# Late cells of a Winograd feed-forward: two tile pairs finished elsewhere, and the last result added on the chip

## The reference

```
def causal_dwconv(x, past, w, b):
    ...
    for k in range(width):
        y = y + w[k] * xp[:, k:k + t]
    return y, xp[:, -(width - 1):]
...
    x = x + jnp.concatenate([o_a, o_m, o_b], axis=-1) @ w_out
    up = rmsnorm(x, g_ffn) @ w_up
    up, f_conv_new = causal_dwconv(up, f_conv_past, conv_f_w, conv_f_b)
    val, gt = jnp.split(up, 2, axis=-1)
    x = x + (jax.nn.gelu(gt) * val) @ w_down
```

## Time and profile before

| what | us |
|---|---|
| median of 3 runs | 2377.11 (2375.92 to 2377.87) |
| the profiled execution, device time | 2379.29 |
| its span, first to last instruction | 2377.5 |
| PE busy | 2320.7 (98%) |
| DVE busy | 1780.0 (75%) |
| ACT busy | 1130.8 (48%) |
| POOL busy | 399.9 (17%) |

### The profile page before, as it was taken

How to read it: one execution, slowest core, us unless ns; L and a number is a source line. 1 busy time by engine, 2 the same in 40 slices (tenths; PEclk the granted TensorE clock), 3 DMA queues, 4 the chain that set the end, 5 groups by cost and what they waited for, 6 DMA issues and landing times.

```text
span 2377.5 us, 45151 instructions
## 1 busy us (share of the span) xinstructions
PE 2320.7 (98%) x18194; PEld 2294.1 (96%) x18194; DVE 1780.0 (75%) x2284; ACT 1130.8 (48%) x1776; POOL 399.9 (17%) x313
## 2 busy tenths in 40 slices
PE   6799999999999999999999999999999899999998
PEld 6799999999999999999999999999999899999998
DVE  7877655655423698888888888888888878787875
ACT  4465433433422355555455555555555545454543
POOL 6500000000022201211112111121211221112121
PEclk9899999999999999999999999999999999999999
DMA  7523333333343343443434434344445568676854
GB/s 231 161 81 83 87 93 99 87 91 92 119 145 110 98 118 115 140 121 109 139 115 131 124 116 130 119 129 121 130 121 156 152 175 209 158 203 169 206 134 89
DMA packets 481733, 309.33 MB, mean 130 GB/s; under 512 B 10744, under 2 KB 459896, under 8 KB 481544
## 3 DMA queue, kind: packets, MB, share of 16 engines
q1 hardware_dynamic: 472824, 288.86, 41.3%
q0 software_dynamic: 8720, 17.83, 4.6%
HBM read 255.23 MB, written 53.51 MB: 130 GB/s over the span
## 4 chain that ended last, share of the span: by engine, by line
PE 91%; DVE 6%; issue 1%; ACT 1%; DMA 1%; POOLq 0%; SPq 0%; DVEq 0%; ACTq 0%
PE out L2358 20%; PE out L2360 20%; PE out L2359 20%; PE out L2064 9%; PE out L2065 9%; PE out L2067 9%; DVE xl L1459 1%; PE out L2200 1%; PE out L2143 1%; DVE ring_l L1793 1%; PE out L2158 1%; DVE wl L1449 1%; DMA raw<-in_w_mem_kv 1%; DVE t L1786 0%; DVE fl L2006 0%
## 5 line engine op out<-in xcount | busy, mean ns | idle before, releaser
L1793 DVE TENSOR_TENSOR ring_l<-pair,ring_h 128x1024 fp32r<-128x1024 f32 (+1 forms) x384 | 453.6, 1182 | 177.1 <-ACT ring_h L1273 177.1
L1273 ACT CAST ring_h<-pair 128x1024 fp32r<-128x1024 f32 (+1 forms) x384 | 383.3, 998 | 325.3 <-DVE pair L1811 240.1
L2064 PE MATMUL out<-xh,wh 128*128 128x272 f32 (+1 forms) x1792 | 504.2, 298 | 29.4 <-DVE xl L1459 25.2
L2065 PE MATMUL out<-xl,wh 128*128 128x272 f32 (+1 forms) x1792 | 488.8, 290 | 0.0
L2358 PE MATMUL out<-t,ring_h 128*128 128x272 f32 x1536 | 445.0, 290 | 6.8 <-DVE ring_l L1793 3.4
L2360 PE MATMUL out<-t,ring_l 128*128 128x272 f32 x1536 | 444.7, 290 | 0.0
L2359 PE MATMUL out<-t,ring_h 128*128 128x272 f32 x1536 | 442.6, 288 | 0.0
L2358 PE MATMUL out<-fh,ring_h 128*128 128x272 f32 x1344 | 390.2, 290 | 7.5 <-DVE fl L2006 3.2
L2360 PE MATMUL out<-fh,ring_l 128*128 128x272 f32 x1344 | 388.7, 289 | 0.0
L2359 PE MATMUL out<-fl,ring_h 128*128 128x272 f32 x1344 | 387.6, 288 | 0.0
L2067 PE MATMUL out<-xh,wl 128*128 128x272 f32 (+1 forms) x1792 | 384.2, 290 | 0.0
(11 more groups left out here) (242 smaller groups left out, 3927.6 us busy)
## 6 DMA issues: line engine op xcount, KB each, us to landing
pair<-in_w_up SPq DMA_DIRECT2D x192, 512.0 KB, 3.9
raw<-in_w_in SPq DMA_DIRECT2D x36, 1024.0 KB, 5.5
pair<-in_w_down SPq DMA_DIRECT2D x64, 384.0 KB, 4.5
pair_d<-in_w_down SPq DMA_DIRECT2D x64, 384.0 KB, 4.7
h_forms<-fb SPq DMA_DIRECT2D x24, 816.0 KB, 6.0
fr<-h_forms SPq DMA_DIRECT2D x24, 816.0 KB, 6.3
out_yT<-stage POOLq DMA_DIRECT2D x31, 544.0 KB, 8.5
raw<-in_w_out SPq DMA_DIRECT2D x16, 1024.0 KB, 5.8
```

The costliest lines, as they stand in the source:

```text
L1273: nc.scalar.copy(ring_h[:, n % 3, 0:width(i)], weight_of(p, i)).then_inc(op_hi, 1)
L1793: v.tensor_tensor(ring_l[:, n % 3, 0:w], weight_of(p, i), ring_h[:, n % 3, 0:w].bitcast(F32), ALU.subtract).then_inc(op_lo, 1)
L2064: mm(dst, w_high, hs, start=first, stop=False)
L2065: mm(dst, w_high, ls, start=False, stop=False)
```

## The change

It has four parts.

1. The value half of pair 46 (`scale_val`, `tap_f(.., 0)`, `conv_f(.., 0)`, `make_h`) leaves cell 47 and goes to cells FT + 1 and FT + 2, with `make_t` for it on POOL in cell FT + 2. In cell 47, form 1 is now split at step 2 instead of step 1.
2. The chain of pair 47 goes one cell later and its end to the end of a cell: `scale_gate`, `scale_val` and the gate's `tap_f` in FT + 3, gate convolution and gelu in FT + 4, value convolution and `make_h` at the end of FT + 5, `make_t` on POOL in FT + 5 behind `make_s3`.
3. Forms 8 and 9 are split in cells FT + 6 (step 0) and FT + 7 (step 0) instead of FT + 5 and FT + 6 (step 5), and form 10 at step 1 instead of step 0 of FT + 7. SP stores `fb` at the end of its cell FT + 6 and loads form 9 right behind it, where before it stored in FT + 5 and loaded at the head of FT + 6.
4. The last cell's output is added in SBUF: SP reads that part of y back (`y_rest`) in cell 74, DVE adds it while it copies PSUM (`kept_with_y`, four operations that take the place of ACT's `keep_a`, `keep_b`, `keep_c`, `read_c21`), and SP stores the sums with three plain transfers in place of POOL's two accumulating ones.

```
-            steps = [(e - 1, 6), (e, 1), (e, 3), (e, 6), (e + 1, 0), (e + 1, 2), (e + 1, 3)]
+            steps = [(e - 1, 6), (e, 2), (e, 3), (e, 6), (e + 1, 0), (e + 1, 2), (e + 1, 3)]
+        if c == 1:
+            steps[1:4] = [(e - 1, 0), (e, 0), (e, 1)]
...
-                if nears == 1:
+                if nears == 1 and g > FT + PAIRS_D:
                     load_form(first + 2)
...
-                if g == FT + 5:
+                if g == FT + 3:
+                    store_b11(FT - 2)
+                if g == FT + 6:
                     store_forms(FT - 1)
+                    load_form(first + 2)
+                if g == FT + PAIRS_D:
                     sp.wait_ge(f_kept, 2 * FT)
...
+                if g == CELLS - 6:
+                    d = CELLS - FT - 1 - PAIRS_D
+                    sp.wait_ge(y_out[1], 16 * (d // 2 + 1))
+                    sp.dma_start(y_rest[:], two_tiles(d)).then_inc(y_back, 16)
+            i = CELLS - 1
+            dst, src = two_tiles(i - FT), stage[(i - FT) % 2]
+            sp.wait_ge(c11_read, i + 1)
+            sp.dma_start(dst[:, 0, 0:HALF], src[:, 0, 0:HALF]).then_inc(last_out, 16)
...
+            sp.wait_ge(c12_read, i + 1)
+            sp.dma_start(dst[:, 0, HALF:ROWS], src[:, 0, HALF:ROWS]).then_inc(last_out, 16)
...
             for g in range(CELLS - 1):
-                if 2 <= g < FT + 1:
+                if 2 <= g < FT:
                     make_t(g - 2)
-                if g == FT + 5:
-                    make_t(FT - 1)
                 if g > FT:
                     add_to_y(g - 1)
                 make_s3(g + 1)
+                if g == FT + 2:
+                    make_t(FT - 2)
+                if g == FT + 5:
+                    make_t(FT - 1)
...
+            def kept_with_y(p, kept, tile, half, ready):
+                i = CELLS - 1
+                dve.wait_ge(product, at(p, i) + 1)
...
+                v.tensor_tensor(kept, x_bank(i), y_rest[:, tile, half * HALF:(half + 1) * HALF], ALU.add
+                                ).then_inc(ready, 1)
...
-                elif g == FT + 4:
-                    conv_f(FT - 1, 0)
-                    make_h(FT - 1)
...
                 make_s4(g + 1)
+                if g == FT + 2:
+                    conv_f(FT - 2, 0)
+                    make_h(FT - 2)
+                if g == FT + 5:
+                    conv_f(FT - 1, 0)
+                    make_h(FT - 1)
                 lo_form(g, 6)
```

More of the change, by code:

```diff
@@ L248, in encoder @@
                  over("stage1", [P, 2, ROWS], x_at + 5 * slot_size)]
-        assert u_at + slot_size <= rows_at + KT * ROWS * 4 and 5 * slot_size + 8 * ROWS <= 8 * form
+        y_rest = over("y_rest", [P, 2, ROWS], u_at + slot_size)
+        assert u_at + slot_size + 8 * ROWS <= rows_at + KT * ROWS * 4 and 5 * slot_size + 8 * ROWS <= 8 * form
         xc, ga, gi, dec, tan = (rows[:, n, :] for n in range(5))
@@ L375, in encoder @@
         y_out = [sem("y_out0"), sem("y_out1")]
+        y_back = sem("y_back")
+        last_out = sem("last_out")
         small_out = sem("small_out")
@@ L446, in tiles_of, with two_tiles @@
             return first, first + 4
+        def two_tiles(d):
+            first, second = tiles_of(d)
+            return yT.rearrange("(k p) n -> p k n", p=P)[:, first:second + 1:second - first, :]
         def x_bank(i):
@@ L775, in _ @@
                     refill(g, 1)
-                if g % 2 and g < FT:
-                    if g == FT - 1:
-                        store_forms(g - 2)
+                if g == FT - 1:
+                    store_forms(g - 2)
+                elif g % 2 and g < FT:
                     store_b11(g - 1)
@@ L925, in add_to_y @@
                     pool.wait_ge(y_out[d % 2], 16 * (d // 2))
[L926 to L934, removed]
+                pool.wait_ge(c11_read, i + 1)
+                pool.wait_ge(c12_read, i + 1)
+                pool.wait_ge(c21_read, i + 1)
+                pool.wait_ge(c22_read, i + 1)
+                nc.gpsimd.dma_start(two_tiles(d), stage[d % 2][:], accum_op=ALU.add).then_inc(y_out[d % 2], 16)
             for g in range(CELLS - 1):
-                if 2 <= g < FT + 1:
+                if 2 <= g < FT:
                     make_t(g - 2)
-                if g == FT + 5:
-                    make_t(FT - 1)
                 if g > FT:
@@ L1275, in keep_a @@
             def keep_a(i):
+                if i == CELLS - 1:
+                    return
                 act.wait_ge(product, at(1, i) + 1)
@@ L1412, in _ @@
                     gelu_f(g - 1)
+                if g < FT - 1:
                     tap_f(g - 1, 0)
-                elif g == FT + 2:
+                elif g == FT + 1:
+                    tap_f(FT - 2, 0)
+                elif g == FT + 3:
                     tap_f(FT - 1, 1)
-                elif g == FT + 3:
+                elif g == FT + 4:
                     gelu_f(FT - 1)
@@ L1429, in _ @@
             g = CELLS - 1
-            hi_op(7, g)
-            keep_b(g)
-            hi_op(4, g)
-            keep_c(g)
-            hi_op(3, g)
-            read_c21(g)
+            for p in (7, 4, 3):
+                hi_op(p, g)
         @block.vector
@@ L2007, in lo_form @@
                                 ).then_inc(form_lo, 1)
+            def kept_with_y(p, kept, tile, half, ready):
+                i = CELLS - 1
+                dve.wait_ge(product, at(p, i) + 1)
+                if p != 4:
+                    dve.wait_ge({1: c11_read, 6: c12_read, 7: c22_read}[p], i)
+                dve.wait_ge(y_back, 16)
+                if p == 4:
+                    dve.wait_ge(y_out[(i - FT) % 2], 16 * ((i - FT) // 2))
+                v.tensor_tensor(kept, x_bank(i), y_rest[:, tile, half * HALF:(half + 1) * HALF], ALU.add
+                                ).then_inc(ready, 1)
             for g in range(1, CELLS - 1):
@@ L2017, in _ @@
                 lo_op(7, g)
-                if g < FT:
+                if g < FT - 1:
                     scale_val(g - 1)
-                elif g == FT + 2:
+                elif g == FT + 1:
+                    scale_val(FT - 2)
+                elif g == FT + 3:
                     scale_val(FT - 1)
@@ L2050, in _ @@
             lo_op(4, g)
+            kept_with_y(6, kept_b[:], 0, 1, b_kept)
             lo_op(3, g)
+            kept_with_y(7, kept_c[:], 1, 1, c_kept)
             read_c22(g)
+            kept_with_y(4, stage[(g - FT) % 2][:, 1, 0:HALF], 1, 0, c21_read)
             read_c12(g)
```

18 lines of the change are left out of this document (11 added, 7 removed).

## The result

The changed kernel takes 2387.43 us, median of 6 runs (2386.21 to 2388.97), against 2377.56 for the kernel before (6 runs). The ratio is 1.0043, 95% interval [1.0030, 1.0056]: 9.9 us slower. The forecast was 2378.8 with a range to 2384, so it was wrong, and on the side of its second rival. The profiled execution took 2388.21 us with a span of 2386.4.

The account below looks back on a forecast made before the run. PE's matmuls are 91% of the chain, so only PE's waits could change. Gains of 11.5 us against costs of 13.2 made it 1.7 longer, 2378.8 us predicted from the 2377.11 median, range 2372 to 2384.

Parts of the forecast that it names:

- second rival: ACT's cast of form 9 in FT + 7: slower store and load, wait 12.2 us, total 2382.7; chance 0.23.
- Part D: Form 9 loaded behind the store: PE waits 8.3 us at product 7 of FT + 7, clock 1.4; cost 9.7.
- part A: Seam at cell 47: DVE bounds it, form 3 starts 3.1 us sooner; gain 4.2, bounds 2.5 and 5.5.
- B: Cell FT + 4: the 2.09 us wait and its clock loss go, product 6 waits 0.7; gain 3.0.
- C: Moved work's new places, ends of FT + 2 and FT + 5: new PE waits; cost 3.5, bounds 2 and 5.
- part E: The end: plain stores from SP, POOL's drain already over; gain 4.1 us, bounds 2.8 and 4.6.
- third rival: The seam yields little: DVE filled by forms 3 to 6 and POOL's s3, gain 2.5, total 2380.5; chance 0.10.
- The 0.2 for forms 8 and 9: Cells after FT + 4: forms 8 and 9 no longer at step 5 of the next two cells; gain 0.2 us.
- Mostly hidden: Rival on the wait for form 9: 3 us or less remains, clock unhurt, total 2371.6; chance 0.22.

Follow-up runs that it names:

- e5: Changed kernel with SP's cell FT + 6 transfers in the order ACT needs: store of fb, form 9, form 10, form 11; 2381.98 us.
- e4: Kernel before with only the change's last part: last cell's additions in SBUF and plain stores; 2373.55 us.
- e1: Kernel before with only SP's store of fb moved to the end of FT + 6 and form 9's load behind it; 2390.14 us.
- e7: Changed kernel with pair 47's second convolution, make_h and make_t one cell earlier, SP's former order, and form 1 at step 1 of cell 47; 2374.15 us.
- e9: Changed kernel with store and form 9's load ahead of forms 10 and 11, and POOL's y additions of FT + 5 and FT + 6 cut to two columns; 2378.38 us.
- e8: Changed kernel with POOL's y additions of cells FT + 5 and FT + 6 cut to two columns; 2383.65 us.

## Why the prediction was wrong

**Part D was mis-sized, not misplaced.** The forecast named the store, the load, ACT's cast of form 9, the 13.12 us wait's exact place and the clock behind it. It put the cost at 9.7; it was 15.4, and that alone takes the sum from 1.7 to 7.4. The other 1.5 of the 8.9 us between the two profiles are 1.9 less gain in part A and 0.5 more cost in parts B and C, less 0.2 in part E and the 0.7 ahead of the change. The step that failed is its last sentence: "I take the medians, since both transfers have the queue nearly to themselves." They had not. By terms, in the order of the chain: PE was due at 1981.3 and not 1983.4, because the parts ahead had gained, but the store went out at the forecast time (1974.78 for 1975.0), since on full queues SP issued the last load of weights in 1.27 us where 0.37 had been enough before, and form 11 in 3.53 and not 2.43: 1.9 more to wait. The store landed after 8.8 us and not 6.0: 2.8 more. Form 9's load took 6.6 us with its issue and not 6.4, and what DVE does behind it 0.1 more than forecast. 8.3 + 1.9 + 2.8 + 0.3 is 13.3, for 13.1 in the trace. The clock cost 1.9 and not 1.4.

**The medians came from another regime.** 23 of the 24 stores of the earlier trace rows are in up cells, in which no y addition exists, and the queues had room: their mean share was 0.81 to 0.86 during the four of these stores issued at 917.7, 1002.0, 1170.5 and 1296.9. The 24th, at 1956.5, went out into queues with a mean share of 0.72:

```profile
1956.50:1962.80 6.30, 6.30 (x52) 6.18 (x50) 5.74 (x6) 3.84 (x5) 1.54 (x1) 1.00 0.72 256
```

The trace of before had the right answer for the new place. From 1968 to 1974 its queues read:

```profile
q0 software_dynamic: 272, 0.56, 53.9%
q1 hardware_dynamic: 1494, 0.81, 50.5%
...
fr<-h_forms SPq DMA_DIRECT2D x2, 816.0 KB, 8.8
```

The form loads issued in that stretch landed after 8.8 us, and the earlier trace rows already showed ACT waiting for one. An addition of 544 KB held 54% of the 16 engines' time for six microseconds here and 60% in the same stretch of the changed kernel; SP's transfers moved with the rest. The Trainium skill (DMA: Bandwidth & Descriptors, SWDGE vs HWDGE vs iDMA) says that software and hardware queues are different queues inside each DMA engine, between which the engine goes round. The shares of the two queues fit that: 53.9 to 50.5% before, 55.8 to 48.5% in e5, 59.9 to 40.5% in the changed kernel. The fit of the Trainium skill (DMA: Bandwidth & Descriptors, Anatomy of one DMA — SWDGE (gpsimd) path), by which the store would take 3.9 us as an estimate, weighed in the forecast and left aside, was further off still. With 8.8 for the store in place of its median, and nothing else changed, part D would have come to 12.5 and the forecast to 2381.6.

**Part A was half its size.** 4.2 was forecast, 2.3 came by the two profiles. Form 3's low part starts at 1856.13 against 1858.72, which is 2.6, of which 0.7 was there before; so 1.9 and not 3.1 sooner. What ate the difference is in DVE's rows above: the 2.35 us of convolution and `make_h` had stood beside POOL's `make_s3`, the taps at their usual 0.78 and 0.79, and with them gone the low part for product 5 stands there and takes 2.44 us in place of 0.95. This is the third rival's mechanism ("DVE is filled by forms 3 to 6 and POOL's s3 whatever is taken out"), and its 2.5 for part A was nearer than my 4.2. And the clock fell after the shorter wait as well. That it "fell after 2.09 and held after 1.89" told nothing: in e4 it fell after 1.88 and held after 2.10. What a fall costs depends on where it comes. From ACT's cast to product 6 of cell 49 pass 44.6 us in the profile of before and 42.3 in that of after; in both it fell behind form 3. In e1 and e4, with the old order, it fell near 1849, where DVE sets the pace and PE has to wait anyway, and the same way took 43.3. The eight executions with the new order took 41.9 to 42.6. So the seam gained 2.3 between the two profiles in which the clock fell at the same place, and 1.0 against e1 and e4; which of the two is usual for the kernel before, three executions with its order can't tell. e7 shows that nothing of it comes from form 1's place.

**Parts B and C were right.** B: the wait went from 2.09 to 0.65 and the clock held, 2.9 with the restart for 3.0. C: 1.08 at FT + 3, 1.06 and 1.29 at FT + 6, with restarts some 3.7 for 3.5. The 0.2 for forms 8 and 9 did not show. POOL's late addition stopped DVE for 0.76 us inside part D, as forecast at no cost. What C lacked was its other price: this late addition, sent at 1965.58, is what the loads ahead of the store meet (it went out 2.6 us sooner in e1, where the wait was 2.9 us shorter). **Part E** was right: 4.3 in the profile, 4.05 in e4, for 4.1.

**The rivals.** The second, "The wait for form 9 is long", was the right one and still short by 4.7 us. "Mostly hidden" falls with the wait of 13.1: even e9, with the best order and without the additions, keeps 3.2. Part D's upper bound, 15.5, held the cost (15.4). The range, which ended at 2384, stopped 0.5 us short of it (2378.8 and 5.7 is 2384.5), because the bound was two slow transfers, and I took these for bad luck rather than for the usual case at that place. The rest of the miss is mostly part A.

## What to carry to other kernels

Take a transfer's time from transfers of the same stretch: look at which queues are busy there before you take the median over the program. When a transfer is moved behind others, its price is its own time, their bytes, and whatever another engine sends meanwhile; and it is paid in full as soon as an engine that executes in order stands in front of it. Work moved off a busy stretch is best cut to fit the new place: whole, it cost 2.9 us more than in two pieces. And before work is moved, look at what another engine does beside it: operations that POOL does not slow may shield, where they stand, those that it does.

## What the runs showed of the hardware

A store of 816 KB that took 6.0 us in the median, in queues with room (shares of 0.72 to 0.86), took 8.7 to 9.3 in full ones, and its time hardly depended on what filled them: two form loads (8.8 in e8) or one addition from POOL (9.3 in e5). Behind weight loads alone it took 7.5 (e9). Full DMA queues also stop the issuing engine: SP needed 3.53 us to issue one load that takes 0.49 in the median, and 1.56 for the same load without the addition (e8).

On DVE a low part, `ring_l` from two operands in SBUF, took 2.44 and 2.47 us beside POOL's `make_s3` where it takes 0.95 without; a tap of the convolution, which reads `conv` in PSUM, took 0.78 or 0.79 in either place.

PE's granted clock fell after some waits of 1.9 us and held after others of 2.1, with the same instructions ahead. It is not a property of the wait alone, and a forecast should carry it as a range, here 0 to 1.4 us for waits of 1.9 to 3.2 us (1.9 behind 13.12, 2.7 behind 5.58).
